# An eight-expert layer's entry re-ordered: a gather that ends bank by bank, three weight remainders on GpSimd, gates computed later, and five identity products at the start

## The reference

```python
def swiglu(h, w_gate, w_up, w_down):
    return (jax.nn.silu(h @ w_gate) * (h @ w_up)) @ w_down

def moe_swiglu(h, router_w, w_gate, w_up, w_down):
    logits = (h @ router_w).astype(f32)
    top_val, top_idx = lax.top_k(logits, TOP_K)
    top_w = jax.nn.softmax(top_val, axis=-1)
    gates = jnp.sum(jax.nn.one_hot(top_idx, N_EXPERTS, dtype=f32) * top_w[..., None], axis=-2)
    y = jnp.zeros_like(h)
    for e in range(N_EXPERTS):
        y = y + gates[..., e:e + 1].astype(h.dtype) * swiglu(h, w_gate[e], w_up[e], w_down[e])
    return y
...
    for l in range(DEPTH):
        h = rms_norm(x, ln_mix[l])
        proj = h @ w_in[l]
        ...
        x = x + (jnp.concatenate([ya, yr], axis=-1) @ w_out[l]).astype(x.dtype)
        h = rms_norm(x, ln_ffn[l])
        y = swiglu(...) if l % 2 == 0 else moe_swiglu(...)
        x = x + y.astype(x.dtype)
    return rms_norm(x, ln_final)
```

## Time and profile before

| | |
|---|---|
| median of three runs | 1098.6 us (1096.19 to 1100.35) |
| profiled execution, its own time | 1103.96 us |
| span of its instructions | 1102.1 us |
| busy share of the span | PE 97%, DVE 64%, ACT 55%, POOL 3% |
| chain that ended last | PE 79%, DMA 13%, DVE 3% |
| DMA over the span | 320 GB/s in the mean |

### The profile page before, as it was taken

How to read it: one execution, slowest core, us unless ns; L and a number is a source line. 1 busy time by engine, 2 the same in 40 slices (tenths; PEclk the granted TensorE clock), 3 DMA queues, 4 the chain that set the end, 5 groups by cost and what they waited for, 6 DMA issues and landing times.

```text
span 1102.1 us, 15644 instructions
## 1 busy us (share of the span) xinstructions
PE 1069.8 (97%) x5449; PEld 808.8 (73%) x5449; DVE 705.7 (64%) x863; ACT 610.3 (55%) x784; POOL 31.4 (3%) x41
## 2 busy tenths in 40 slices
PE   8999999999999989999989999999999999999995
PEld 6887888888788768884447888886448888888341
DVE  5777555554677689971038989994009999997111
ACT  6645544443563378760038878883018888875102
POOL 0200000000001000000000000000000000000000
PEclk9999999999999999989999999999999999999999
DMA  9974559555454349989999999999999999999994
GB/s 337 365 237 153 191 189 331 176 185 194 147 187 159 133 140 366 351 310 354 412 410 408 409 410 410 407 401 385 405 414 410 403 414 410 402 416 393 387 414 174
DMA packets 115375, 352.72 MB, mean 320 GB/s; under 512 B 7380, under 2 KB 36276, under 8 KB 107040
## 3 DMA queue, kind: packets, MB, share of 16 engines
q1 hardware_dynamic: 112752, 341.16, 81.4%
q0 software_dynamic: 2144, 9.92, 2.5%
q10 hardware_dynamic: 400, 0.63, 0.2%
HBM read 348.36 MB, written 8.78 MB: 324 GB/s over the span
## 4 chain that ended last, share of the span: by engine, by line
PE 79%; DMA 13%; DVE 3%; SPq 2%; issue 1%; ACT 1%; ACTq 0%; DVEq 0%; POOLq 0%
PE psum L1585 76%; DMA raw<-in_exp_w_down 6%; DMA raw<-in_exp_w_gate 3%; PE psum L1582 3%; DMA back<-scratch 2%; SPq L682 2%; DMA bucket_sb<-const_buckets 1%; DMA scratch<-oe,row_e 1%; DVE w_lo L574 1%; DVE prob L1248 1%; ACT w_hi L590 0%; DVE x_sb L1413 0%; DVE w_lo L597 0%; DVE x_sb L1151 0%; DVE psums L1240 0%
## 5 line engine op out<-in xcount | busy, mean ns | idle before, releaser
L597 DVE TENSOR_TENSOR w_lo<-raw,w_hi 128x1024 fp32r<-128x1024 f32 x330 | 393.4, 1222 | 68.5 <-ACT w_hi L590 35.7
L590 ACT ACTIVATE w_hi<-raw 128x1024 fp32r<-128x1024 f32 x330 | 342.3, 1060 | 100.1 <-PE psum L1585 61.2
L1585 PE MATMUL psum<-w_hi,aT_hi 128*128 128x512 f32 (+1 forms) x900 | 336.9, 380 | 8.7 <-DVE aT_lo L1138 3.3
L1585 PE MATMUL psum<-w_hi,aT_lo 128*128 128x512 f32 (+1 forms) x900 | 332.1, 374 | 0.0
L1585 PE MATMUL psum<-w_lo,aT_hi 128*128 128x512 f32 (+1 forms) x900 | 242.6, 375 | 2.1 <-DVE w_lo L597 1.6
L1585 PEld LDWEIGHTS psum<-w_hi,aT_hi 128*128 128x128 f32 x900 | 170.5, 189 | 41.1 <-issue 4.7
L1585 PEld LDWEIGHTS psum<-w_hi,aT_lo 128*128 128x128 f32 x900 | 170.6, 190 | 28.9
L1585 PEld LDWEIGHTS psum<-w_lo,aT_hi 128*128 128x128 f32 x900 | 161.8, 189 | 35.6 <-DVE w_lo L597 5.2
L574 DVE TENSOR_TENSOR w_lo<-raw,w_hi 128x1024 fp32r<-128x1024 f32 x118 | 145.3, 1239 | 44.6 <-PE psum L1585 44.1
L565 ACT ACTIVATE w_hi<-raw 128x1024 fp32r<-128x1024 f32 x118 | 124.1, 1059 | 88.9 <-PE psum L1585 85.2
L1585 PE MATMUL psum<-raw,aS 128*64 128x512 f32 (+3 forms) x624 | 118.9, 534 | 0.0
(11 more groups left out here) (231 smaller groups left out, 726.9 us busy)
## 6 DMA issues: line engine op xcount, KB each, us to landing
raw<-in_exp_w_down SPq DMA_DIRECT2D x88, 1024.0 KB, 16.9
raw<-in_exp_w_gate SPq DMA_DIRECT2D x64, 1024.0 KB, 16.1
raw<-in_exp_w_up SPq DMA_DIRECT2D x64, 1024.0 KB, 15.4
raw<-in_exp_w_gate SPq DMA_DIRECT2D x24, 768.0 KB, 11.2
raw<-in_exp_w_up SPq DMA_DIRECT2D x24, 768.0 KB, 11.0
raw<-in_w_in SPq DMA_DIRECT2D x17, 1024.0 KB, 6.2
raw<-in_ffn_w_gate SPq DMA_DIRECT2D x22, 512.0 KB, 3.9
raw<-in_ffn_w_up SPq DMA_DIRECT2D x22, 512.0 KB, 5.0
```

The source lines that it names most:

```text
L590: nc.scalar.activation(w_hi[:, q % HIGHS, :], raw_piece(slot, q % 2), ACT.Copy).then_inc(hi_made, 1)
L597: eng.tensor_tensor(w_lo[:, q % LOWS, :], raw_piece(e_slot[s][q // 2], q % 2), w_hi[:, q % HIGHS, :].bitcast(F32), ALU.subtract).then_inc( ...
L1585: return pe.matmul(dst, a, b, start=start, stop=stop, skip_group_check=True)
```

## The change

It has five parts. (1) `gather` makes the four groups of high products first as before, by token tile, but then the low products bank by bank, so that bank after bank is complete; the second bank is now PSUM bank 4 in place of 1, since piece 0 of expert 0 writes banks 0 and 1. (2) Expert 0's first product waits for one bank only, pieces 2, 4 and 6 for the others; DVE makes all four low parts of the tokens in a row. (3) The first three weight remainders of expert 0 move from DVE to GpSimd, behind its instructions for `info`. (4) The gates move behind the four low parts and behind a wait for GpSimd's three remainders. (5) Behind the first turning of tokens PE makes five products of the identity with itself.

```diff
+GATHER_BANKS = (0, 4, 2, 3)
...
-START_BUSY = 7
+START_BUSY, HOLD_BUSY = 7, 5
...
@@ GpSimd
             pool.tensor_tensor(info[:, :, :, 0], one, ...).then_inc(info_rows, 1)
+            for q in range(LOWS):
+                low_part_e(pool, 0, 0, q)
             pool.wait_ge(route_ready, 1)
...
@@ ScalarE, VectorE: gather_high, gather_low
-                got = bank(b).rearrange("p (k t) -> p k t", k=2)
+                got = bank(GATHER_BANKS[b]).rearrange("p (k t) -> p k t", k=2)
...
@@ VectorE
             dve.tensor_scalar(passes_i[:], passes_f[:], 1.0, None, ALU.add).then_inc(route_ready, 1)
-
-            dve.wait_ge(e2_made, 1)
-            link(dve.tensor_scalar(total, e2, 1.0, None, ALU.add))
...
-            dve.tensor_tensor(info[:, :, :, 1], gates, tmp, ALU.add).then_inc(info_ready, 1)
...
-                for q in range(1 if e == 0 else 0, LOWS):
+                for q in range(0 if e > 0 else LOWS, LOWS):
                     low_part_e(dve, r, e, q)
...
-                    if e in INFO_IN and q < 2:
+                    if 0 < e and e in INFO_IN and q < 2:
                         gather_low(r, INFO_IN[e], 2 + q)
...
-            for b in range(2):
+            for b in range(4):
                 gather_low(0, 0, b)
-            low_part_e(dve, 0, 0, 0)
+            dve.wait_ge(lo_vec, FRONT_PIECES + LOWS)
+            dve.wait_ge(e2_made, 1)
+            link(dve.tensor_scalar(total, e2, 1.0, None, ALU.add))
...
+            dve.tensor_tensor(info[:, :, :, 1], gates, tmp, ALU.add).then_inc(info_ready, 1)
...
@@ TensorE
                 turn_h(2 * layer)
+                if layer == 0:
+                    for again in range(HOLD_BUSY):
+                        mm(psum[:, 4, 0:P], ident, ident, True, True)
...
-                for part, t in ((0, 0), (0, 1), (1, 0), (1, 1)):
...
+                for t in range(TT):
+                    for k in range(DK):
+                        add(k, 0, t)
+                for b in range(DK // 2):
+                    for t in range(TT):
                         pe.wait_ge(xg_lo_made, t + 1)
+                        for k in (2 * b, 2 * b + 1):
+                            ins = add(k, 1, t)
+                    ins.then_inc(gathered, 1)
...
-                    if e in INFO_IN and q in (0, 4, 6):
+                    if e in INFO_IN and q in (0, 2, 4, 6):
...
-                        pe.wait_ge(g_hi, highs(r, INFO_IN[e]) + {0: 2, 4: 3, 6: 4}[q])
+                        pe.wait_ge(g_hi, highs(r, INFO_IN[e]) + (q // 2 + 1))
...
@@ small experts, before their gather
-                        pe.wait_ge(e_hid, chunks(r, s) + NS)
+                        pe.wait_ge(e_hi, chunks(r, s) + NS)
```

More of the change, by code:

```diff
@@ L1542, in vec_small @@
                                                  op0=ALU.mult, op1=ALU.mult).then_inc(e_hid, 1)
-            for b in range(2):
+            for b in range(4):
                 gather_low(0, 0, b)
-            low_part_e(dve, 0, 0, 0)
+            dve.wait_ge(lo_vec, FRONT_PIECES + LOWS)
+            dve.wait_ge(e2_made, 1)
+            link(dve.tensor_scalar(total, e2, 1.0, None, ALU.add))
+            link(dve.reciprocal(part1, total))
+            link(dve.tensor_tensor(part2, e2, part1, ALU.mult))
+            link.also(dve.tensor_tensor(gates, hot1, wide(part1), ALU.mult))
+            link(dve.tensor_tensor(tmp, hot2, wide(part2), ALU.mult))
+            dve.tensor_tensor(info[:, :, :, 1], gates, tmp, ALU.add).then_inc(info_ready, 1)
             with dve.Fori(0, n_pass) as r:
@@ L1552, in _ @@
                     mark_slots(place_of, r, 0)
-                    for b in range(2):
+                    for b in range(4):
                         gather_low(r, 0, b)
-                    low_part_e(dve, r, 0, 0)
+                    for q in range(LOWS):
+                        low_part_e(dve, r, 0, q)
                 with dve.Else():
@@ L1854, in gather, with add @@
                 pe.wait_ge(picked, marked(r, g))
-                for part, t in ((0, 0), (0, 1), (1, 0), (1, 1)):
-                    if part == 1:
-                        pe.wait_ge(xg_lo_made, t + 1)
[L1858 to L1864, removed]
+                def add(k, part, t):
+                    dst = psum[:, GATHER_BANKS[k // 2], (k % 2) * SEQ:(k % 2) * SEQ + last - first]
+                    tokens = (xg_lo if part else xg_hi)[:, t, k * P:(k + 1) * P]
+                    return mm(dst, tokens, pick[:, t, first:last], part == t == k % 2 == 0, part == t == k % 2 == 1)
+                for t in range(TT):
[3 more added lines that the diff above has]
+                    for t in range(TT):
+                        pe.wait_ge(xg_lo_made, t + 1)
+                        for k in (2 * b, 2 * b + 1):
+                            ins = add(k, 1, t)
+                    ins.then_inc(gathered, 1)
             def gather_info(r, g):
```

6 lines of the change are left out of this document (1 added, 5 removed).

## The result

The changed kernel took 1104.96 us in the median of seven runs (1103.03 to 1107.12), the kernel before 1098.6 us beside it; the ratio is 1.0049, with a 95% interval of 1.0036 to 1.0062. That is 5.4 us, above the 4.35 of the sum, and on the edge between the forecast's "within" 0.5% and its "slower". The profiled execution of the changed kernel took 1104.96, with a span of 1103.1.

What follows compares the result with a forecast made beforehand. Expert-weight DMA was taken to bound 510 to 1085 us, with entry shifts passing to the end one for one. -1.2 (start) + 5.55 (entry) = +4.35 on 1098.6 gave 1103; range 1095.5 to 1106, the forecast's own 1101 to 1105.

Steps and rivals of the forecast that it cites:

- front, until `pick`: Program start: identity products fill PE's idle time, its clock stays at 2.4 GHz; -1.2 us, bounds 0 and -1.7.
- `pick` to `passes_i`: Expert 0's entry: GpSimd's remainders take turns with `xg_lo` and the step before `passes_i`, which comes 6.15 us later.
- `passes_i` to ACT's start: Expert 0's entry: ACT's start follows `passes_i` by 1.47 us as before, so the bank-by-bank gather is worth nothing.
- one bank (ACT's start to PE's): Expert 0's first product waits for one low part instead of two; PE starts about 0.6 us earlier, 1.57 behind ACT.
- PE's start to piece 2: Expert 0's first pieces: the same clock fall and the same 5.27 us; bounds -1.7 and +0.9.
- the turns are between GpSimd and those of DVE's instructions that have two inputs in SBUF: Expert 0's entry: whole instructions alternate, holding `xg_lo` but not `pick`; forecast chance 0.55.
- the slow rival: Entry: `pick` takes turns with the remainders too; expert 0 starts +7.0, sum +5.8, 1104.4 us; chance 0.21.
- `pick` over 2 us: Sign in the profile after, at the entry: if `pick` takes more than 2 us, the rival with `pick` held holds.
- The row of 220 ns against 171: One-input TENSOR_SCALAR L1121, like `pick`, stretched once beside GpSimd's L781; the trace's only evidence that `pick` is held.
- The clock at the entry: PE idles 3.6 us instead of 2.49 before expert 0; same clock fall expected, bound -1.7 if none.
- The gates: Made later, done at 408.3, wanted by PE behind piece 1 at 410.0: hidden; at full clock the cover nearly vanishes.
- One for one: A shift at expert 0's entry moves the DMA slots behind it, the transfers and the end by the same amount.

Runs made afterwards that it cites:

- second trace of before: The unchanged kernel before, traced once more; span 1096.6 us, near its median, with no half clock at the start or at the gather near 486.
- e6: The changed kernel with GpSimd waiting until the four picks are made before its three remainders; 1104.35 us, ratio 1.0042 to the kernel before.
- first trace of before: The unchanged kernel before, in the profiled execution the prediction read; span 1102.1 us, one of its long executions.
- e9: The kernel before with a delay alone, five of the six pass-count steps repeated four more times; 1101.75 us, ratio 1.0028.
- e5: The changed kernel with GpSimd's three remainders made behind its wait for the pass count; 1102.64 us, ratio 1.0039 to the kernel before.
- the second of after: The changed kernel, unchanged, traced once more; span 1101.5 us, same starts at the entry to 0.02 us, clock fall at 1006 but not 489.
- e3: The kernel before with expert 0's first three remainders alone moved to GpSimd; 1104.67 us, ratio 1.0057.
- e8: The changed kernel without GpSimd's remainders, pass-count steps in front of `xg_lo`, gates behind the low part of bank 0; 1097.72 us, ratio 0.9978 to the kernel before.
- e7: The changed kernel with the remainders back on DVE and the gates early; 1098.59 us, ratio 0.9992 to the kernel before.
- e11: The kernel with the pass count first and no GpSimd remainders, later experts' gathers cut in two; 1096.2 us, ratio 0.9970 to the kernel before.

## Why the prediction was right, and by which wrong step

**The time** lay in the range and, at 1104.96, just within the forecast's own range (1101 to 1105), and the direction was right. The delay at the entry, from the second trace of before to after, as it stands at piece 2:

| step | predicted | measured |
|---|---|---|
| front, until `pick` | -1.2 | -0.38 (391.04 to 390.66; in the nine traces with the products 389.60 to 390.99) |
| `pick` to `passes_i` | +6.15 | +6.32 (3.77 to 10.09) |
| `passes_i` to ACT's start | 0 | -0.01 |
| one bank (ACT's start to PE's) | -0.6 | -0.60 (2.17 to 1.57) |
| PE's start to piece 2 | 0 | -1.59 (5.25 to 3.66) |
| sum | +4.35 | +3.74 |

**The step that failed** is "the turns are between GpSimd and those of DVE's instructions that have two inputs in SBUF". `pick` has one, and was held: 4.1 of the 6.3 are `pick`'s, only 2.2 are `xg_lo`'s, and the pass count's steps, which I had held for the rest, were not (in the trace of after the third remainder had ended before them). That `pick` is held is the slow rival's mechanism, and its sign (`pick` over 2 us) came in; its price, +7.0 at the first product, was too high (measured +5.71 behind `pick`, 7.57 to 13.28). Two picks slipped through GpSimd's wait for `w_hi`, so all four took 5.00 where the rival had 7.9, and expert 0 then followed `passes_i`, not the gather at half clock as the rival had it. Nor are the holds turns: in e6 DVE's two `xg_lo` ran back to back and GpSimd waited for both. That the forecast's +6.15 came so near the 6.32 is luck. It let three remainders each hold one step of DVE's, and three did, but other steps than it named; in e6, where another one is first, the same three remainders cost 4.0. The row of 220 ns against 171, for a two-column instruction, was right, and I gave it too little. The rule of the Trainium skill that I quoted beside the rival ("VectorE: DVE Perf Modes", "The perf-mode tier table", which gives float32 tensor_scalar from SBUF a doubled rate, and that rate both ports) has `pick` held, and the 2.30 and 2.38 agree with it.

**The identity products** seem to hold the clock: there is no fall at the start in nine traces with them, and there are two in four without (the first trace of before and e9). Four traces are few, and the idle time alone does not tell them apart: the clock fell after 2.23 idle in e9 and did not after 2.40 in the second trace of before. The -1.2 was the price of a fall that happened in the execution I read, and not in every one. The timed effect is 1.0004 with an interval of about 0.13% on either side; an average gain of half a microsecond would not show.

**The clock at the entry** I took as unchanged, with a bound of -1.7: it fell earlier, while PE waited for `pick` (half clock from 393.6 to 400.4), and had risen again when expert 0 began. The bound was met almost in full, -1.6.

**The gates** were hidden, as said: `info` ended at 406.46, PE came to it at 406.79 without idling. "The cover is all but gone" is borne out too: in e5, where GpSimd began later, it was gone and cost 0.57.

**One for one.** This step held in the main. The 3.74 at piece 2 is 3.81 at the gather near 1004, from the second trace of before to the second of after. Of the pure delay of 2.86 in e9 the time kept 3.1, within a wide interval; its trace starts the first of these gathers 4.48 later than the second trace of before and the second one 3.48 later, so 1.0 was made up there.

The changed kernel's 5.4 is more than its 3.74. For the execution that was profiled first the traces show one reason: the fall of the clock at 489, by which it was 2.13 later at 1004 than the second. The prediction had no term for that. That such falls make the rest of the 5.4 in the timed runs is likely and not shown: with the later gathers cut the loss is 3.4 (0.0031 x 1099), but the intervals overlap. The mean clock of 0.9897, against 0.992 to 0.993 of before, proves less than it seems, since some half of the difference is, by the traces, the longer half clock at the entry (6.8 us in place of 3.4), which the 3.74 already holds. Nor do the traces show that falls at those gathers come oftener behind a later entry: uncut, four of five traces with a late entry have one (the two of after, e3, e6; not e9), and four of six of the others. Why they come stays open, and so does the upper group of runs in e5 and e9.

## What to carry to other kernels

GpSimd is not a free engine beside VectorE: a remainder of 2.35 us put beside small VectorE steps on the critical path can cost nearly its whole length at each place where it gets in first, even against a step of 0.16 us. Before moving work to another engine, ask what the waiting engine really waits for: here it was a register read of the pass count, and with six small steps moved forward expert 0 came to piece 2 2.4 earlier against `pick` (9.79 in e8, 12.22 in e7), which is what the change sought, without GpSimd. One profiled execution can hold events (a clock fall) that the median lacks; a term that is read from such an event is worth its share only, and a second trace of the kernel before shows whether it is one.

## What the runs showed of the hardware

- Which VectorE steps a GpSimd tensor_tensor of 128x1024 kept out: TENSOR_SCALAR of 128x128 (2.30, alone 0.88 for four) and of 128x6 (2.38 against 0.16), TENSOR_TENSOR (3.40 against 1.22), SCALAR_TENSOR_TENSOR of 128x1 (1.94 against 0.16). Not kept out: TENSOR_REDUCE and TENSOR_SCALAR of 128x1, 0.15 each, and TENSOR_TENSOR of 128x512 with one input in PSUM (four in 2.48 beside the remainders of e5, 2.49 alone in the trace of after).
- GpSimd is kept out in turn: 4.45 in place of 2.33, while two VectorE instructions of 1.2 ran back to back. Nothing alternated between those two.
- From the pass count's start to ScalarE's first instruction behind its register read it took 1.62 or 1.63 in eleven traces, wherever the count stood; only where the gather came later than that (e8, e11) it took more.
- PE's clock fell to its lower level in the middle of a full stretch, with PE busy all the time, at 32 gather products of 64 columns that take 3.6 us together, and only in some executions (eight of the eleven traces with these products uncut). One such fall, of 3.4 us, made what follows some 2 us later (1004.71 against 1002.58).
